# Expert rows by indirect DMA through a slot table, and a third full weight buffer, in one decoder layer with 32 experts

## The chip, the cores and the metric

The kernel runs on one core of one Trainium2 chip. The core has a matrix engine (TensorE, written PE; PEld is its weight load), a vector engine (DVE), an activation engine (ACT), GpSimd (POOL) and SyncE (SP), which issues DMAs. Transfers that SP, ACT and POOL issue run on the same 16 DMA engines. The metric is the device time of one execution in microseconds (us). Time before: median 947.78 us of 3 runs, 944.93 to 948.92. About 0.5% is what a measurement of this kernel can tell from no change.

## What is computed

One layer of a hybrid decoder: RMSNorm, one input projection, four parallel mixers, an output projection with a residual, then a second RMSNorm and a mixture of experts with a residual. 512 prompt tokens and 8 sample tokens pass through, 520 in all; everything is float32. The change concerns the mixture of experts and what stands just ahead of it. Each token picks one group of experts and two experts in it; there are 32 experts, each with a 1024x1024 matrix of gate and up columns (4 MB) and a 512x1024 matrix down (2 MB).

```python
D_MODEL = 1024; N_GROUPS = 4; EXP_PER_GROUP = 8; N_EXPERTS = 32; TOP_E = 2; D_EXPERT = 512
...
def moe_ffn(x, wg_r, bg_r, we_r, be_r, w_gu, w_down):
    ...
    gsel = jnp.argmax(lg, axis=-1)
    p_group = jnp.take_along_axis(pg, gsel[:, None], axis=-1)
    ...
    tv, ti = lax.top_k(le_g, TOP_E)
    gate = p_group * jax.nn.softmax(tv, axis=-1)
    eidx = gsel[:, None] * EXP_PER_GROUP + ti
    return expert_dispatch(xt, eidx, gate, w_gu, w_down).reshape(B_, L, D)
...
    # per expert e, over the tokens xi that chose it:
        a, b = jnp.split(xi @ w_gu[e], 2, axis=-1)
        return (jax.nn.silu(a) * b) @ w_down[e]
...
    return jax.ops.segment_sum(yb * buf_gate[:, None].astype(yb.dtype), buf_tok, num_segments=T)
```

## The kernel before

Every engine has its own instruction stream, written out by hand; semaphores (`S["..."]`, waited for with `wait_ge`) are the only order between streams. An engine works in the order of its stream, so what stands behind a wait waits too. Tokens lie on partitions in five tiles: four of 128 prompt tokens and one of 8 sample tokens. Large regions of SBUF (`reg_a`, `reg_b`, `reg_w`, `reg_h`, `reg_x`, `reg_y`, `reg_q`) are reused from stage to stage.

The work ahead of the experts ends with the output projection (weights in `reg_w`), the second norm (its result `h2` lies in `reg_h`), the router's logits and, on DVE, the choice of experts. `mask_bf` says which token chose which expert; PE multiplies it with triangular and full matrices of ones, and `pos` is then a token's place in its expert's list. An expert takes up to `CAP` = 64 tokens in one round; the number of rounds is computed on the chip (`n_rounds`), and in the profile it is one.

The expert loop on PE (`expert`, L1424 to L1452). A list of 64 tokens with 1024 numbers each is kept as 128 partitions of 512: the first half of a row on partitions 0 to 63, the second on 64 to 127, and matmuls come in pairs, one for each half of the array. For expert n PE does

- 16 matmul calls of gate and up (bank 2 or 3), in four parts; a part begins when its quarter of the weights has landed (`gu_loaded`), and its end frees that quarter (`gu_part_done`);
- 8 calls of `gather` for the expert after it: the tokens' rows are fetched by multiplying a one-hot matrix (made by DVE, `make_onehot`, L1876) with `h2`; the last 2 calls, of the tile with the sample tokens, stand after the next item;
- the transposition of `hid`, silu(gate) times up (ACT L1013, DVE L1925), which DVE copies into `hT` (L1929);
- 8 calls of the down projection with `hT`, and in the middle of them `turn_tokens`, 4 transpositions of the rows that `gather` fetched (ACT copies them out of the bank first), which DVE copies into `xe` (`copy_xe`, L1916).

A matmul call in float32 stands as two records in the profile. Line L1031 is the helper of all matmuls, L1034 that of all transpositions, L731 that of ACT's copies.

Weights: SP issues four DMAs of 1 MB for an expert's gate and up matrix (`load_gu`, L559) and one of 2 MB for the down matrix (`load_down`, L564). Three places hold gate and up matrices (`reg_a`, `reg_b`, `reg_w`), two hold down matrices (`reg_a`, `reg_b`). Experts 0 and 1 are loaded under the output projection, the gate and up matrix of expert 2 once the output projection has left `reg_w`. The third place is used for experts 2 and 5 alone; from expert 6 on the loop alternates between `reg_a` and `reg_b`. Each load waits for PE to have freed its place.

ACT copies an expert's result `y_out` and stores it in two DMAs into `expert_rows` in DRAM, 64 rows whether filled or not (L1022). After the last store POOL fetches, for every token, the rows of its two experts with ten indirect DMAs (L724; `slot_u` holds the row numbers), and DVE adds them to the residual, weighted by `gate` (L1943, ten operations); SP stores each finished tile.

## Time and profile before

| what | value |
|---|---|
| median of 3 runs | 947.78 us (944.93 to 948.92) |
| the profiled execution | 949.59 us |
| its span | 947.9 us |
| PE busy | 868.7 us, 92% |
| DVE, ACT, POOL busy | 242.0, 174.3, 65.1 us |
| mean granted clock of PE | 0.957 |
| DMA | 249.48 MB, 263 GB/s over the span |

The profiled execution took 949.59 us, 1.7 us more than its span and 1.8 us more than the median. PE's busy time counts a matmul from its issue to its modelled end, so full occupancy says that PE always had work queued, not that it could not be faster. From about 407 us to 917 us PE runs the expert loop; the DMA share (1.00 is all 16 DMA engines busy) and GB/s by stretch tell how the weights came in beside it. The order of instructions that is quoted below gives line, operation, out<-in and shape; a row with xN stands for N equal ones, and the rows ISA and REGISTER_ALU are an engine's own bookkeeping for loops and semaphores.

### The profile page before, as it was taken

The numbers are of one execution on the slowest core, as the hardware profiler recorded it, in microseconds if no ns is written. First come the engines' busy times: TensorE is split into PE (matmuls) and PEld (weight loads), VectorE is DVE, ScalarE is ACT, GpSimd is POOL, SyncE is SP. The second block draws the span as 40 slices with busy tenths as digits, with TensorE's granted clock in tenths as the row PEclk, the third lists the DMA queues.
The fourth block names the chain that finished last, engine by engine and source line by source line (L and its number), as shares of the span: only waits on it lengthen the run. The fifth ranks groups of instructions, "written<-read, shape, count | busy, mean of one in ns | idle before, by whom it ended". The sixth has DMA issues, their size and how long they took to land.

```text
span 947.9 us, 11251 instructions
## 1 busy us (share of the span) xinstructions
PE 868.7 (92%) x4270; PEld 439.6 (46%) x4270; DVE 242.0 (26%) x576; ACT 174.3 (18%) x386; POOL 65.1 (7%) x96
## 2 busy tenths in 40 slices
PE   4999899979889999599999999999999999999960
PEld 3787588848658455333333333333333333333320
DVE  3322004348668221611111111111111111110105
ACT  4113213021354301111111111111111111101100
POOL 6011000241100000000000000000000000000004
PEclk9999899989898999599999999999999999999995
DMA  9722833100600670459997999999999999999717
GB/s 300 122 62 67 265 126 95 50 19 1 268 1 1 264 293 4 174 194 410 401 381 284 397 412 400 425 411 415 396 426 405 422 396 424 406 423 409 289 27 265
DMA packets 69266, 249.48 MB, mean 263 GB/s; under 512 B 16772, under 2 KB 36115, under 8 KB 44619
## 3 DMA queue, kind: packets, MB, share of 16 engines
q1 hardware_dynamic: 62705, 234.12, 63.7%
q10 hardware_dynamic: 5314, 10.68, 3.0%
q0 software_dynamic: 1216, 4.26, 1.4%
q8 instruction: 20, 0.33, 0.1%
q14 instruction: 11, 0.09, 0.0%
...
## 4 chain that ended last, share of the span: by engine, by line
PE 83%; DVE 9%; DMA 2%; issue 2%; POOL 1%; ACT 1%; SPq 1%; POOLq 0%; ACTq 0%; DVEq 0%
PE bank L1031 76%; PE bank L1034 6%; POOL reg_a L724 1%; DMA reg_x<-in_x_prompt 1%; DMA reg_a<-expert_rows,slot_u 1%; DVE reg_a L1687 1%; DVE reg_a L1767 1%; DVE reg_a L1677 0%; DVE reg_x L1677 0%; DVE small L1728 0%; DMA reg_a<-in_state_win_kv 0%; POOL small L662 0%; DVE reg_a L1679 0%; DVE reg_a L1696 0%; POOLq L179 0%
## 5 line engine op out<-in xcount | busy, mean ns | idle before, releaser
L1031 PE MATMUL bank<-reg_a,reg_y 128*64 128x512 f32 x736 | 166.6, 594 | 0.9 <-DVE reg_y L1916 0.9
L1031 PE MATMUL bank<-reg_b,reg_y 128*64 128x512 f32 x736 | 166.5, 594 | 0.0
L1031 PE MATMUL bank<-reg_h,reg_y 128*64 128x512 f32 x660 | 156.2, 603 | 1.6 <-DVE reg_y L1876 1.6
L1031 PEld LDWEIGHTS bank<-reg_a,reg_y 128*64 128x64 f32 x736 | 51.8, 137 | 98.7 <-issue 96.5
L1031 PEld LDWEIGHTS bank<-reg_b,reg_y 128*64 128x64 f32 x736 | 51.8, 137 | 98.2 <-issue 96.0
L1031 PE MATMUL bank<-reg_b,reg_w 128*128 128x260 f32 x384 | 85.3, 383 | 0.0
L1031 PEld LDWEIGHTS bank<-reg_h,reg_y 128*64 128x64 f32 x660 | 45.1, 138 | 82.1 <-issue 78.2
L1925 DVE TENSOR_TENSOR reg_y<-reg_y,bank 128x256 f32<-128x256 f32 x32 | 13.5, 421 | 270.2 <-ACT reg_y L1013 270.2
L1031 PEld LDWEIGHTS bank<-reg_b,reg_w 128*128 128x128 f32 x384 | 72.7, 190 | 12.1 <-issue 1.1
L1031 PE MATMUL bank<-reg_w,reg_y 128*128 128x512 f32 (+2 forms) x256 | 75.8, 570 | 0.0
L731 ACT ACTIVATE reg_y<-bank 128x512 f32<-128x512 f32 x49 | 29.3, 597 | 213.8 <-PE bank L1031 213.8
L1031 PE MATMUL bank<-reg_w,reg_b 128*128 128x256 f32 (+2 forms) x320 | 60.5, 382 | 0.0
L1031 PEld LDWEIGHTS bank<-reg_w,reg_b 128*128 128x128 f32 (+1 forms) x320 | 50.8, 170 | 8.3 <-ACT reg_a L731 0.4
L724 POOL DMA_INDIRECT reg_a<-expert_rows,slot_u x10 | 13.5, 1350 | 543.8 <-ACTq L1025 541.1
L1034 PEld LDWEIGHTS bank<-small,reg_y 128*128 128x128 f32 (+3 forms) x209 | 25.3, 159 | 54.2 <-issue 52.3
L1031 PEld LDWEIGHTS bank<-reg_w,reg_y 128*128 128x128 f32 (+2 forms) x256 | 30.3, 157 | 39.9 <-issue 39.1
L1916 DVE COPY reg_y<-bank 128x512 f32<-128x512 f32 x33 | 22.9, 692 | 94.3 <-PE bank L1034 94.3
L1013 ACT ACTIVATE reg_y<-bank 128x256 f32<-128x256 f32 x32 | 12.3, 385 | 154.0 <-PE bank L1031 154.0
L1034 PE MATMUL bank<-small,reg_y 128*128 128x128 f32 (+3 forms) x209 | 39.9, 300 | 0.7 <-ACT reg_y L731 0.7
L1929 DVE COPY reg_y<-bank 128x256 f32<-128x256 f32 x32 | 13.6, 425 | 83.8 <-PE bank L1034 83.8
L662 POOL TENSOR_TENSOR small<-small 128x1 f32<-128x1 f32 (+4 forms) x18 | 20.2, 1126 | 199.2 <-DVE small L1821 68.1
L1034 PE MATMUL bank<-small,reg_h 128*128 128x128 f32 (+1 forms) x108 | 17.7, 315 | 16.0 <-DVE reg_h L1479 13.8
...
## 6 DMA issues: line engine op xcount, KB each, us to landing
reg_a<-in_exp_w_gu SPq DMA_DIRECT2D x60, 1024.0 KB, 12.1
reg_b<-in_exp_w_gu SPq DMA_DIRECT2D x60, 1024.0 KB, 12.4
reg_a<-in_exp_w_down SPq DMA_DIRECT2D x16, 2048.0 KB, 10.7
reg_b<-in_exp_w_down SPq DMA_DIRECT2D x16, 2048.0 KB, 10.5
reg_w<-in_w_in SPq DMA_DIRECT2D x9, 1024.0 KB, 10.4
reg_w<-in_exp_w_gu SPq DMA_DIRECT2D x8, 1024.0 KB, 11.8
...
expert_rows<-reg_y ACTq DMA_DIRECT2D x32, 128.0 KB, 7.7
```

Of the source, the lines that this page charges most:

```text
L662: eng.tensor_tensor(out, in_, minus_half[0:out.shape[0], 0:out.shape[-1]], ALU.pow).then_inc(S[s_done], 1)
L724: eng.indirect_dma_start(dst, None, y_dram[:, :], bass.IndirectOffsetOnAxis(ap=slot_u[0:ROWS[i], 5 * k + i:5 * k + i + 1], axis=0)).then_i ...
L731: return eng.activation(out, in_, ACT.Copy)
L1013: eng.activation(silu[b], bank[2 + b][:, 0:256], ACT.Silu).then_inc(S["silu_done"], 1)
L1031: return eng.matmul(out, lhsT, rhs, start=start, stop=stop, skip_group_check=True)
L1034: return eng.transpose(out, in_, ident[0:in_.shape[0], 0:in_.shape[0]])
L1687: link(eng.reciprocal(u, u))
L1767: eng.reciprocal(rs, rs).then_inc(S["nrm_made"], 1)
L1916: eng.tensor_copy(xe[b], bank[1][:, :].rearrange("p (j s n) -> p j s n", j=4, s=2)).then_inc(S["xe_made"], 1)
L1925: tt(hid[b], silu[b], bank[2 + b][:, 256:512], ALU.mult).then_inc(S["hid_made"], 1)
L1929: eng.tensor_copy(hT[b], bank[4 + b][:, 0:256].rearrange("p (k s) -> p k s", k=2)).then_inc(S["hT_made"], 1)
```

## The change

- PE no longer fetches tokens with one-hot matmuls. ACT stores `h2` into DRAM (`ffn_in`) tile by tile. DVE makes a table of which token's half-row belongs on which of the 128 partitions for each expert (`find_slots`, ten small bf16 matmuls `slot_table`, `rows_of_slots`); partitions without a token get a number that the bounds check drops. POOL fetches an expert's rows from `ffn_in` into `xe_rows` with one indirect DMA (`gather`).
- Results go from `y_out` into `expert_rows` with one indirect DMA an expert, issued by POOL (`scatter`); `expert_rows` now has a row for each token and choice, and at the end plain DMAs bring it back (`combined_rows`, by SP and ACT), two rows a token at once.
- `reg_h`, free once `h2` is stored and transposed, becomes the third place for down matrices. Expert e uses place e mod 3; the down matrix of expert 2 is loaded ahead of the loop too.
- Constants for the table are added to POOL's first work.

The expert loop on PE, two experts in a row of the loop of before (names: `small` holds the identity matrix of a transposition, `reg_h` is `h2`):

```order
L1031 MATMUL bank<-reg_a,reg_y 64x512 x16
L1435 REGISTER_ALU
L1031 MATMUL bank<-reg_h,reg_y 64x512 x8
L1034 MATMUL bank<-small,reg_y 128x128 x2
L1031 MATMUL bank<-reg_h,reg_y 64x512 x2
L1442 ISA
L1031 MATMUL bank<-reg_a,reg_y 64x512 x4
L1034 MATMUL bank<-small,reg_y 128x128 x4
L1031 MATMUL bank<-reg_a,reg_y 64x512 x4
```

The same loop of now, its second and third expert (`reg_h` is here a down matrix):

```order
L1068 MATMUL bank<-reg_b,reg_y 64x512 x16
L1443 REGISTER_ALU
L1071 MATMUL bank<-small,reg_y 128x128 x6
L1068 MATMUL bank<-reg_b,reg_y 64x512 x8
L1459 REGISTER_ALU
L1463 ISA
L1068 MATMUL bank<-reg_w,reg_y 64x512 x16
L1071 MATMUL bank<-small,reg_y 128x128 x6
L1068 MATMUL bank<-reg_h,reg_y 64x512 x8
```

The ten calls of `gather` are gone; the four transpositions of the next expert's rows moved from the middle of the down projection to just behind gate and up, ahead of the two of `hid`.

DVE ahead of the loop, before, from the mask of chosen experts to the first one-hot matrices:

```order
L1866 CAST mask_bf<-reg_y 128x160
L1869 COPY reg_y<-bank 128x160
L1872 SCALAR_TENSOR_TENSOR reg_q<-reg_y 128x5x32
L1873 TENSOR_SCALAR reg_q<-reg_q 128x5x32
L1876 TENSOR_TENSOR reg_y<-small,reg_q 128x320 x2
```

The same place now, up to the matrix for `slot_table` (128x1280) and the first step of the round count:

```order
L1895 CAST mask_bf<-reg_y 128x160
L1897 TENSOR_SCALAR reg_q<-reg_y,small 128x10x32
L1898 TENSOR_TENSOR reg_q<-reg_y,small 128x5x32
L1899 TENSOR_TENSOR reg_q<-reg_y,small 128x5x32
L1900 MEMSET reg_q 128x5x16
L1901 CAST reg_q<-reg_y 128x5x32
L1904 COPY reg_y<-bank 128x160
L1906 TENSOR_TENSOR reg_y<-reg_y 128x320
L1907 TENSOR_REDUCE reg_q<-reg_y 128x10
L1911 TENSOR_TENSOR reg_q<-small,reg_q 128x1280
L1930 TENSOR_REDUCE reg_y<-bank 128x1
```

Five operations on the token numbers came in ahead of the copy of `pos`, and the places of the tokens (L1906, L1907) moved ahead of the loop's first fetch.

POOL behind the norms, before (`slot_u` holds row numbers, `reg_a` takes the rows):

```order
L717 TENSOR_LOAD n_rounds
L717 ISA x2
L718 UNCONDITIONAL_BRANCH
L718 ISA
L724 DMA reg_a<-expert_rows,slot_u 128x1024 x2
L724 DMA reg_a<-expert_rows,slot_u 8x1024 x2
L724 DMA reg_a<-expert_rows,slot_u 128x1024 x6
```

And now, for the first two of 32 experts (`reg_q` holds the row numbers, `reg_y` the fetched rows and one of the two result buffers):

```order
L736 TENSOR_LOAD n_rounds
L736 ISA x2
L747 UNCONDITIONAL_BRANCH
L747 ISA
L741 DMA reg_y<-ffn_in,reg_q 128x512 x2
L755 ISA
L741 DMA reg_y<-ffn_in,reg_q 128x512
L758 REGISTER_ALU
L745 DMA expert_rows<-reg_y,reg_q 2080x512
L755 REGISTER_ALU
L741 DMA reg_y<-ffn_in,reg_q 128x512
L758 REGISTER_ALU
```

Ten indirect DMAs after the loop became 64 inside it, a fetch for expert e+2 and a return for expert e in turn.

The core of the diff:

```diff
-        down_w = [r.t[:, 8192:12288].rearrange("p (s c n) -> p s c n", s=2, c=2) for r in (reg_a, reg_b)]
+        down_w = [r.t[:, at:at + 4096].rearrange("p (s c n) -> p s c n", s=2, c=2) for r, at in ((reg_a, 8192), (reg_b, 8192), (reg_h, 0))]
...
+        h2_dram = nc.dram_tensor("ffn_in", [T, D], F32, kind="Internal").ap()
+        y_dram = nc.dram_tensor("expert_rows", [2 * T, D], F32, kind="Internal").ap()
...
+        USES = [11, 11, 10]
+        h2_halves = h2_dram.rearrange("t (s n) -> (t s) n", s=2)
+        y_halves = y_dram.rearrange("t (s n) -> (t s) n", s=2)
+        y_pairs = y_dram.rearrange("(k t) d -> t k d", k=2)
+        def combined_rows(eng, t):
+            q = ROWS[t]
+            dst = reg_a.t[0:q, 2 * t * D:2 * t * D + 2 * D].rearrange("p (k d) -> p k d", k=2)
+            eng.dma_start(dst, y_pairs[COL[t]:COL[t] + q]).then_inc(y_back[t], 16)
...
-                for e, g in ((3, 0), (4, 1), (5, 2), (6, 0), (7, 1)):
-                    load_gu(e, g, first + e - 2)
-                    load_down(e - 1, (e - 1) % 2, first + e - 2)
-                with eng.Fori(0, (N_EXP - 8) // 2) as i:
-                    for k in range(2):
-                        e = 2 * i + 7 + k
-                        load_down(e, 1 - k, first + e - 1)
-                        load_gu(e + 1, k, first + e)
-                load_down(N_EXP - 1, 1, first + N_EXP - 2)
+                with eng.Fori(1, N_EXP // 3) as i:
+                    for g in range(3):
+                        e = 3 * i + g
+                        load_gu(e, g, first + e - 2)
+                        load_down(e, g, first + e - 2)
+                for e in range(N_EXP - N_EXP % 3, N_EXP):
+                    load_gu(e, e % 3, first + e - 2)
+                    load_down(e, e % 3, first + e - 2)
...
+            eng.wait_ge(S["h2_stored"], 16 * NTILE)
+            eng.wait_ge(bank_full[bank_of["hTb3"]], turn_of["hTb3"] + 1)
+            load_down(2, 2)
...
+            eng.wait_ge(S["round_scattered"], rounds)
+            for t in COMBINE_TILES[0::2]:
+                combined_rows(eng, t)
...
+            eng.wait_ge(S["h2_stored"], 16 * NTILE)
+            def gather(e):
+                idx = bass.IndirectOffsetOnAxis(ap=row_of[:, e:e + 1], axis=0)
+                eng.indirect_dma_start(xe_rows[e % 2], None, h2_halves, idx, bounds_check=2 * T - 1, oob_is_err=False).then_inc(x_gathered[e % 2], 16)
+            def scatter(e):
+                idx = bass.IndirectOffsetOnAxis(ap=row_of[:, N_EXP + e:N_EXP + e + 1], axis=0)
+                eng.indirect_dma_start(y_halves, idx, y_out[e % 2], None, bounds_check=4 * T - 1, oob_is_err=False).then_inc(y_scattered[e % 2], 16)
...
-                eng.sem_inc(S["gather_begun"], 1)
-                for i in COMBINE_TILES:
-                    for k in range(2):
-                        dst = reg_a.t[0:ROWS[i], (2 * i + k) * D:(2 * i + k + 1) * D]
-                        eng.indirect_dma_start(dst, None, y_dram[:, :], bass.IndirectOffsetOnAxis(ap=slot_u[0:ROWS[i], 5 * k + i:5 * k + i + 1], axis=0)).then_inc(rows_gathered[k][i], 16)
+                n = N_EXP * r
+                eng.wait_ge(S["idx_made"], r + 1)
+                eng.sem_inc(S["gather_asked"], 1)
+                gather(0)
+                gather(1)
+                for e in range(N_EXP):
+                    if e + 2 < N_EXP:
+                        eng.wait_ge(S["xe_turned"], n + e + 1)
+                        eng.sem_inc(S["gather_asked"], 1)
+                        gather(e + 2)
+                    eng.wait_ge(S["y_copied"], n + e + 3)
+                    eng.sem_inc(S["scatter_asked"], 1)
+                    scatter(e)
+                for b in range(2):
+                    eng.wait_ge(y_scattered[b], 16 * (N_EXP // 2) * (r + 1))
+                    eng.sem_inc(S["scatter_asked"], 1)
+                eng.sem_inc(S["round_scattered"], 1)
...
+                eng.wait_ge(S["h2_made"], n + 1)
+                eng.dma_start(h2_dram[COL[i]:COL[i] + r], h2[0:r, i, :]).then_inc(S["h2_stored"], 16)
...
+            def expert(e, n, b, reused=None):
+                eng.wait_ge(S["gu_done"], n + 1)
+                eng.activation(silu[b], bank[2 + b][:, 0:256], ACT.Silu).then_inc(S["silu_done"], 1)
+                eng.wait_ge(S["down_done"], n + 1)
+                if reused is not None:
+                    eng.wait_ge(y_scattered[b], reused)
+                copy(y_out[b], bank[6 + b][:, :]).then_inc(S["y_copied"], 1)
...
-                        copy(y_out[b], bank[6 + b][:, :]).then_inc(S["y_copied"], 1)
-                        eng.wait_ge(S["y_copied"], n + 3)
-                        for s in range(2):
-                            eng.dma_start(y_dram[bass.ds(e * CAP, CAP), 512 * s:512 * s + 512], y_out[b][CAP * s:CAP * s + CAP, :]).then_inc(y_stored[b], 16)
...
-            def gather(b, tiles):
-                for t in tiles:
-                    for s in range(2):
-                        ins = mm(bank[0][64 * s:64 * s + 64, :], onehot[b][:, t, :], h2[:, t, 512 * s:512 * s + 512], t == 0, t == NTILE - 1)
-                if t == NTILE - 1:
-                    ins.then_inc(S["gathered"], 1)
...
+            def slot_table(made):
+                eng.wait_ge(S["in_slot_made"], made)
+                for m_ in range(10):
+                    ins = mm(bank[0][:, 0:96], in_slot[:, m_, :], ids[:, m_ // 5, m_ % 5].rearrange("p f e -> p (f e)"), m_ == 0, m_ == 9)
+                ins.then_inc(S["table_made"], 1)
+            def turn_tokens(b, gathered):
+                eng.wait_ge(x_gathered[b], gathered)
                 for j in range(4):
-                    ins = turn(bank[1][:, 128 * j:128 * j + 128], x_tok[:, 128 * j:128 * j + 128])
+                    ins = turn(bank[1][:, 128 * j:128 * j + 128], xe_rows[b][:, 128 * j:128 * j + 128])
                 ins.then_inc(S["xe_turned"], 1)
...
-                eng.wait_ge(S["onehot_made"], n + 2)
-                gather(1 - b, range(4))
+                if gathered is not None:
+                    turn_tokens(1 - b, gathered)
                 eng.wait_ge(S["hid_made"], n + 1)
                 for k in range(2):
                     ins = turn(bank[4 + b][:, 128 * k:128 * k + 128], hid[b].rearrange("p (f k) -> p f k", k=2)[:, :, k])
                 ins.then_inc(S["xt_turned"], 1)
-                gather(1 - b, [4])
-                eng.wait_ge(down_loaded[b], down_loads)
+                eng.wait_ge(down_loaded[g], loads)
                 eng.wait_ge(S["hT_made"], n + 1)
                 eng.wait_ge(S["y_copied"], n + 1)
                 for s_in in range(2):
-                    if s_in == 1:
-                        eng.wait_ge(S["x_tok_made"], n + 2)
-                        turn_tokens()
                     for k in range(2):
...
+            ts(ids[:, :, :, 0], oh, row_one, None, ALU.mult)
+            tt(ids[:, 0, :, 1], oh[:, 0], tile_iota.unsqueeze(2).to_broadcast([128, 5, N_EXP]), ALU.mult)
+            tt(ids[:, 1, :, 1], oh[:, 1], tile_iota.unsqueeze(2).to_broadcast([128, 5, N_EXP]), ALU.mult)
+            eng.memset(ids[:, 0, :, 2], 0.0)
+            eng.tensor_copy(ids[:, 1, :, 2], oh[:, 1])
...
-            link(stt(posm[:, :, 0:N_EXP], pos, 1.0, mask, ALU.add, ALU.mult))
-            link(ts(posm[:, :, 0:N_EXP], posm[:, :, 0:N_EXP], -1.0, None, ALU.add))
-            def make_onehot(n, b):
-                tt(onehot[b], cap_iota.unsqueeze(1).to_broadcast([128, 5, CAP]), posm[:, :, bass.ds(n, 1)].to_broadcast([128, 5, CAP]), ALU.is_equal).then_inc(S["onehot_made"], 1)
-            make_onehot(0, 0)
-            make_onehot(1, 1)
...
+            def find_slots(at):
+                tt(in_slot, cap_iota.unsqueeze(1).to_broadcast([128, 10, 2 * CAP]), at.unsqueeze(2).to_broadcast([128, 10, 2 * CAP]), ALU.is_equal).then_inc(S["in_slot_made"], 1)
+            def rows_of_slots(made, steps):
+                eng.wait_ge(S["table_made"], made)
+                row, tile, second = [bank[0][:, 32 * f:32 * f + 32] for f in range(3)]
+                eng.tensor_copy(slot_no, row).then_inc(S["idx_steps"], 1)
+                eng.wait_ge(S["idx_steps"], steps + 1)
+                stt(slot_v[:, 0], tile, 128.0, slot_no, ALU.mult, ALU.add).then_inc(S["idx_steps"], 1)
+                eng.wait_ge(S["idx_steps"], steps + 2)
+                ts(slot_no, slot_v[:, 0], 0.0, 8192.0, ALU.is_equal, ALU.mult)
+                stt(slot_v[:, 1], second, float(T), slot_v[:, 0], ALU.mult, ALU.add).then_inc(S["idx_steps"], 1)
+                eng.wait_ge(S["idx_steps"], steps + 3)
+                stt(slot_v, slot_v, 2.0, slot_no.unsqueeze(1).to_broadcast([128, 2, N_EXP]), ALU.mult, ALU.add).then_inc(S["idx_steps"], 1)
+                eng.wait_ge(S["idx_steps"], steps + 4)
+                ts(row_of, slot_v.rearrange("p x e -> p (x e)"), half_less2, None, ALU.add).then_inc(S["idx_made"], 1)
+            find_slots(pk10)
...
+            rows_of_slots(1, 0)
...
+                n = N_EXP * r
+                eng.wait_ge(S["idx_made"], r + 1)
+                ts(pk_next, pk_next, float(-CAP), None, ALU.add).then_inc(S["next_at"], 1)
+                eng.wait_ge(S["next_at"], r + 1)
+                find_slots(pk_next)
+                copy_xe(n, 0)
...
+                eng.wait_ge(S["round_scattered"], r + 1)
+                rows_of_slots(r + 2, 4 * r + 4)
+                eng.sem_inc(S["round_open"], 1)
+            for n, t in enumerate(COMBINE_TILES):
+                q = ROWS[t]
+                eng.wait_ge(y_back[t], 16)
+                for k in range(2):
+                    ins = stt(x1[0:q, t, :], reg_a.t[0:q, (2 * t + k) * D:(2 * t + k + 1) * D], gate[0:q, k, t:t + 1], x1[0:q, t, :], ALU.mult, ALU.add)
+                    ins.then_inc(S["half_added" if k == 0 else "y_tile_done"], 1)
+                    if k == 0:
+                        eng.wait_ge(S["half_added"], n + 1)
```

## Rows read from the trace of the kernel before

**Rows 1.** The page: span, and the chain that ended last by line.

```profile
span 947.9 us, 11251 instructions
...
PE bank L1031 76%; PE bank L1034 6%; POOL reg_a L724 1%; DMA reg_x<-in_x_prompt 1%; DMA reg_a<-expert_rows,slot_u 1%; DVE reg_a L1687 1%; DVE reg_a L1767 1%; DVE reg_a L1677 0%; DVE reg_x L1677 0%; DVE small L1728 0%; DMA reg_a<-in_state_win_kv 0%; POOL small L662 0%; DVE reg_a L1679 0%; DVE reg_a L1696 0%; POOLq L179 0%
```

**Rows 2.** Timeline of one expert: start us, us, engine, line, operation, count [idle before].

```profile
605.20 3.60 PE L1031 MATMUL bank<-reg_h,reg_y 128*64 128x512 f32 x16
...
605.83 0.42 DVE L1925 TENSOR_TENSOR reg_y<-reg_y,bank 128x256 f32<-128x256 f32 x1 [8.47 <-ACT reg_y L1013]
...
608.73 0.50 PE L1034 MATMUL bank<-small,reg_y 128*128 128x128 f32 x2
...
611.89 0.66 PE L1034 MATMUL bank<-small,reg_y 128*128 128x128 f32 x4
...
614.25 7.04 PE L1031 MATMUL bank<-reg_b,reg_y 128*64 128x512 f32 x32
...
621.12 3.60 PE L1031 MATMUL bank<-reg_h,reg_y 128*64 128x512 f32 x16
```

**Rows 3.** Busy time by stretch, with granted clock, DMA share, GB/s.

```profile
core 0: us, PE busy (x) PEld busy (x) DVE busy (x) ACT busy (x) POOL busy (x), PEclk, DMA share, GB/s
...
320.00:340.00 20.00, 20.00 (x68) 9.14 (x67) 7.13 (x8) 2.58 (x6) 1.10 (x2) 1.00 1.01 426
...
380.00:390.00 10.00, 7.86 (x40) 7.32 (x40) 2.94 (x9) 1.84 (x4) 0.48 (x1) 0.60 0.94 395
390.00:400.00 10.00, 2.00 (x24) 1.20 (x26) 8.80 (x57) 0.43 (x2) 0.00 (x0) 0.50 0.01 2
...
500.00:600.00 100.00, 100.00 (x468) 34.41 (x466) 12.34 (x25) 13.92 (x22) 0.00 (x0) 1.00 0.96 386
...
700.00:800.00 100.00, 100.00 (x468) 34.21 (x462) 12.47 (x26) 13.71 (x22) 0.00 (x0) 1.00 1.01 412
```

**Rows 4.** DMA queues (packets, MB, share) and issues (count, KB each, us to landing).

```profile
q10 hardware_dynamic: 5314, 10.68, 3.0%
q0 software_dynamic: 1216, 4.26, 1.4%
...
reg_a<-in_exp_w_gu SPq DMA_DIRECT2D x60, 1024.0 KB, 12.1
...
reg_a<-in_exp_w_down SPq DMA_DIRECT2D x16, 2048.0 KB, 10.7
```

**Rows 5.** Timeline ahead of the loop and at its first matmuls, columns as rows 2.

```profile
395.18 0.56 DVE L1863 TENSOR_TENSOR reg_y<-reg_y,small 128x160 f32<-128x160 f32 x2
...
396.14 0.24 DVE L1866 CAST mask_bf<-reg_y 128x160 bf16<-128x160 f32 x1
...
398.07 0.89 DVE L1876 TENSOR_TENSOR reg_y<-small,reg_q 128x320 f32<-128x320 f32 x2
...
401.19 0.15 DVE L1891 CAST n_rounds<-reg_y 128x1 int32<-128x1 f32 x1
...
407.28 7.09 PE L1031 MATMUL bank<-reg_a,reg_y 128*64 128x512 f32 x32 [0.87 <-DVE reg_y L1916]
...
409.25 5.48 SPq L559 DMA_DIRECT2D reg_a<-in_exp_w_gu  x4
```

**Rows 6.** Timeline of the end, columns as rows 2.

```profile
916.88 0.60 ACT L731 ACTIVATE reg_q<-bank 128x512 f32<-128x512 f32 x1 [3.57 <-PE bank L1031]
...
921.55 1.25 POOL L724 DMA_INDIRECT reg_a<-expert_rows,slot_u  x1 [541.07 <-ACTq L1025]
923.11 0.94 POOL L724 DMA_INDIRECT reg_a<-expert_rows,slot_u  x1 [0.30 <-issue]
...
926.22 1.28 DVE L1943 SCALAR_TENSOR_TENSOR reg_x<-reg_a,reg_q,reg_x 128x1024 f32<-128x1024 f32 x1 [10.06 <-DMA reg_a<-expert_rows,slot_u]
...
928.64 1.99 POOL L724 DMA_INDIRECT reg_a<-expert_rows,slot_u  x1 [0.31 <-issue]
...
943.51 1.28 DVE L1943 SCALAR_TENSOR_TENSOR reg_x<-reg_a,reg_q,reg_x 128x1024 f32<-128x1024 f32 x1 [1.24 <-DMA reg_a<-expert_rows,slot_u]
```

191 lines of the change are left out of this document (78 added, 113 removed).

## The prediction

> **What bounds the kernel now.** I read the page first: the chain that ended last is 76% matmuls, more than half of it the expert loop [rows 1]. Then the timeline of one expert: the same matmuls stand 15.92 us apart (605.20 to 621.12) [rows 2], and 407.28 + 32 x 15.92 = 916.7 us is where the loop ends, 0.2 us before ACT's last copy [rows 5, 6]. PE never waits in it. Third, busy time by stretch, which shows that the transfers have hardly more room: from 700 to 800 us the DMA share is 1.01 at 412 GB/s, PE busy 100.00 [rows 3]. An expert's weights are 4 x 1024 + 2048 KB = 6.29 MB [rows 4], its stored rows 0.26 MB, and 6.55 MB in 15.92 us is that 412. So PE is the bound and the transfers come a few per cent behind. Around the loop stand 407 us ahead of it, which the change touches only at the end, and 31.0 us behind it (916.88 to 947.9) [rows 1, 6].
>
> **PE's work per expert.** Gate and up are 32 records in 621.12 - 614.25 = 6.87 us, 0.2147 each [rows 2]. The ten calls of gather are 20 records, 4.29 us: 15.92 - 4.29 = 11.63. But the gather covered two waits. Until hid is made 1.05 us pass after the last gate-and-up matmul (605.20 to 606.25) [rows 2]; the four moved transpositions (0.66) cover most, 0.4 shows, and since they no longer stand in the middle of the down projection nothing waits there. Behind the transposition of hid the last gather calls (4 records, 0.86) covered the copy into hT; now 0.6 to 1.0 us is open, as DVE copies xe first. Together about 13.0 us an expert (bounds 11.6 to 13.6). If the weights were there, 32 experts would take 416 us.
>
> **The transfers take over.** The weights alone ran at 426 GB/s from 320 to 340 us [rows 3]: 6.29 MB in 14.8 us. Rows: 520 tokens in two experts each are 1040 rows, 32.5 an expert, fetched and returned in halves of 2 KB, so 130 packets if the bounds check drops the empty ones at no cost. Queue q10, which carries the stores of before, took 3.0% of 16 engines x 947.9 us for 5314 packets, 86 ns each [rows 4]: 130 x 86 ns / 16 = 0.7 us. That is 15.5 us an expert, the lower bound. The upper one is the stretch 700 to 800, with 128 such packets in each 15.92 us and no DMA engine idle [rows 3]: 15.9. I take 15.8, nearer to the stretch with this mix of traffic. PE with 13.0 waits for weights from about expert 9 on.
>
> **Where the gain is.** Hardly in 15.92 against 15.8, but in the count: experts 0 to 2 lie in SBUF when the loop begins (down 2 is new, and loads while DVE routes, 390 to 400 us, DMA share 0.01 [rows 3]), so 29 experts are paid at the transfers' rate, and PE is not 16 us behind them at the end.
>
> **Ahead of the loop.** The mask is made at 396.38 [rows 5].
> - Five operations on token numbers: two 160 wide take 0.56 [rows 5], so 1.3 us, while PE makes pos: 397.7.
> - Copy of pos, product, reduction: 0.35 + 0.5 + 0.5, estimated from the 320 wide ones [rows 5]: 399.1.
> - The 1280 wide find_slots: two 320 wide take 0.89 [rows 5], so 1.6: 400.7.
> - Round count, beside the ten matmuls: five steps like n_rounds (0.15 and a gap) [rows 5], 1.1: 401.8. Then rows_of_slots, six steps of about 0.2: 403.1.
> - Two paths to the first transposition. POOL: 4.7 us from an indirect DMA's start to the first sum that used it (921.55 to 926.22) [rows 6], 407.8. DVE: gates 1.1, a register load (no row; 0.5 taken, 0 to 1.9 possible), find_slots again 1.7, then PE's second table about 1.0 and a latency: 407.9. Then 0.66 [rows 2] and the copy into xe, 0.8.
> The loop begins at 409.9 instead of 407.28 (bounds 408.5 to 412). The gather of before also woke the clock; granted 0.50 from 390 to 400 us [rows 3], PE now begins cold, and its first quarter takes 1.7 us more. First buffer free: before 1.97 after the loop's start [rows 5], now 409.9 + 1.97 + 1.7 = 413.6.
>
> The five stores of h2 stand on ACT's queue behind copies that wait for PE anyway, and 2.1 MB of them ride beside loads that nothing awaits before 407 us; SP waits for them ahead of down 2 with nothing else to issue. POOL's extra constants, about 0.7 us before its first power, are put at 0.3 here and dropped.
>
> **The sum.** 413.6 + 2.2 until bytes land (4.67 less POOL's 1.25 and half a MB's 1.2 [rows 6]) + 29 x 15.8 = 874.0. The last down projection, 16 records, 3.4, and a latency: ACT's copy at 877.9 instead of 916.88, 39.0 us earlier. Behind it: copy 0.6, scatter on POOL 1.25 and 3.4 to land, 5.3 in all. Plain loads: issue and latency 2.7, 5 us until the first tile is there (it shares the engines with a second queue), then DVE is the bound: ten sums of 1.28 [rows 6], 12.8, and the last store 3.1 (944.79 to 947.9). 28.9 instead of 31.0, 2.1 gained; bounds 26 to 32, as loads land earlier or later. Span 947.9 - 39.0 - 2.1 = 906.8; the execution 949.59 gives 908.5, and against the median of 947.78, which is 1.8 lower, **906.7, so 907 us**.
>
> **A rule against it.** Of POOL's ten indirect DMAs one that DVE left alone took 0.94 us, one beside DVE's sums 1.99 [rows 6]. The Trainium skill, page "SBUF — State Buffer", section "Who interferes with whom", says that a vector operation in a two-port mode keeps GpSimd from the port it writes descriptors through. By it the first gather and the last scatter would each cost about 1.1 us more, and the sum would be 909; inside the loop POOL has 13 us to spare and nothing changes.
>
> **Rivals.**
> - *Empty rows are not free* (slower). Were all 256 half-rows of the two indirect DMAs moved, and each cost what a packet of POOL's queue q0 did, 1.4% x 947.9 x 16 / 1216 = 175 ns [rows 4], rows would take 2.8 us an expert on every DMA engine: 14.8 + 2.8 = 17.6, and 907 + 29 x 1.8 = 959. It decides from 907 + 29 x 1.4, that is 17.2 us an expert. For it: POOL's queue has never run beside the weights here. Against: q0's packets were twice as long.
> - *Transfers at their slower stretch.* From 500 to 600 us 386 GB/s [rows 3]: 6.29 MB in 16.3, with rows 17.0: 907 + 35 = 942, a gain of only 0.6%. Against: the share there was 0.96, so the engines were not full. Half of that, 16.4, gives 924.
> - *The clock.* PE will wait some 3 of 15.8 us. From 380 to 390 us it was busy 7.86 of 10 and got 0.60 [rows 3], which stands for part of the time at 1.2 GHz. If the down projection always ran at that level, 3.4 us more make 16.4 an expert and PE the bound: 924. Worse is not stable, since a PE that falls behind has no gaps. The Trainium skill, page "TensorE: Matmul & The Clock Gate", section "HAM oscillation", describes this for waits on DMA, each stretch of work starting cold; the stretch just quoted agrees.
> - *A late gather.* Gather e+2 stands on POOL's queue behind scatter e-1, which waits for ACT's copy; it is needed after gate and up of e+1, some 25 us later. At 12.1 us, the longest median landing under load [rows 4], it is hidden; from 25 on it is not. Priced with the first rival.
> - *No change.* The loads were nearly full before, so if 29 paid experts cost 17.1 each, 945.
>
> **Chances.** Forecast (15.4 to 16.1 us an expert, 893 to 916) 0.62; slower transfers or the clock (916 to 943) 0.23; a tail and rate better than taken (below 893) 0.03; no change (943 to 952) 0.04; slower by the first rival 0.08. Faster 0.62 + 0.23 + 0.03 = 0.88, within 0.5% (about what a measurement of this kernel can tell) 0.04, slower 0.08. Range: low end 15.5 an expert (-8.7), an early loop and a short tail (-7): 891; high end 938, inside the slower cases, which leaves out some 0.16.
>
> **What would show it.** In the profile after: DMA share at 1.0 from about 415 to 872 us, gate and up at intervals of 15.8 us with PE idle 2 to 3 us ahead of the down projection; SP's waits for PE shrinking to the first experts; the loop's start at 409 to 412; from ACT's last copy to the end about 29 us, DVE's sums without gaps. Wrong if PE is still busy throughout, if PE waits for x_gathered (the four transpositions late), or if the interval is above 17 us.

## The result

The changed kernel takes 908.51 us (median of 4 runs, 906.86 to 912.16), the kernel before 946.36 us in the runs beside it: ratio 0.9593, 95% interval 0.9557 to 0.9629. A second set of runs gave 909.86 us and 0.9603 (0.9586 to 0.9620). Forecast were 907 us and a range of 891 to 938. The profiled execution spans 905.1 us, where 906.8 was forecast.

### The profile page after: what moved, and what is told of

Same layout as the page of the kernel before. It is cut to its first block, busy times and chain, and to the rows that moved or that the text cites. A ratio compares the mean times of both kernels' runs of the same rounds, so it can differ in the third digit from the quotient of the medians.

```text
span 905.1 us, 9802 instructions
## 1 busy us (share of the span) xinstructions
PE 752.3 (83%) x3626; PEld 404.3 (45%) x3626; DVE 226.2 (25%) x540; ACT 135.3 (15%) x338; POOL 118.9 (13%) x154
## 4 chain that ended last, share of the span: by engine, by line
PE 40%; SPq 34%; DVE 11%; DMA 9%; issue 4%; ACT 2%; POOL 0%; DVEq 0%; ACTq 0%; POOLq 0%
PE bank L1068 37%; SPq L571 28%; DMA reg_b<-in_exp_w_down 7%; SPq L576 5%; PE bank L1071 3%; DVE reg_x L1983 1%; DMA reg_x<-in_x_prompt 1%; DVE reg_a L1718 1%; DMA reg_a<-expert_rows 1%; DVE reg_a L1798 1%; DVE reg_a L1708 1%; DVE reg_x L1708 0%; DVE small L1759 0%; POOL small L681 0%; DVE reg_a L1710 0%
## 5 line engine op out<-in xcount | busy, mean ns | idle before, releaser
L1068 PE MATMUL bank<-reg_a,reg_y 128*64 128x512 f32 x528 | 127.2, 634 | 16.1 <-DMA reg_a<-in_exp_w_down 12.9
L1068 PE MATMUL bank<-reg_b,reg_y 128*64 128x512 f32 x528 | 122.2, 608 | 21.9 <-DMA reg_b<-in_exp_w_down 17.2
L1068 PE MATMUL bank<-reg_w,reg_y 128*64 128x512 f32 (+2 forms) x512 | 134.2, 581 | 4.3 <-DMA reg_w<-in_exp_w_gu 4.3
L1957 DVE TENSOR_TENSOR reg_y<-reg_y,bank 128x256 f32<-128x256 f32 x32 | 13.5, 421 | 421.3 <-ACT reg_y L1047 421.3
L1068 PEld LDWEIGHTS bank<-reg_w,reg_y 128*64 128x64 f32 (+2 forms) x512 | 49.2, 146 | 82.3 <-issue 65.1
L1068 PE MATMUL bank<-reg_b,reg_w 128*128 128x260 f32 x384 | 85.3, 383 | 0.0
L1068 PEld LDWEIGHTS bank<-reg_a,reg_y 128*64 128x64 f32 x528 | 41.2, 145 | 92.7 <-issue 75.6
L1068 PEld LDWEIGHTS bank<-reg_b,reg_y 128*64 128x64 f32 x528 | 39.9, 140 | 94.8 <-issue 64.6
L1068 PEld LDWEIGHTS bank<-reg_b,reg_w 128*128 128x128 f32 x384 | 72.7, 190 | 12.1 <-issue 1.1
L1068 PE MATMUL bank<-reg_h,reg_y 128*64 128x512 f32 x160 | 48.9, 768 | 19.1 <-DMA reg_h<-in_exp_w_down 17.4
L1068 PE MATMUL bank<-reg_w,reg_b 128*128 128x256 f32 (+2 forms) x320 | 60.5, 382 | 0.0
L1068 PEld LDWEIGHTS bank<-reg_w,reg_b 128*128 128x128 f32 (+1 forms) x320 | 50.8, 170 | 8.3 <-ACT reg_a L771 0.4
L1071 PEld LDWEIGHTS bank<-small,reg_y 128*128 128x128 f32 (+3 forms) x205 | 25.2, 161 | 45.8 <-issue 25.5
L745 POOL DMA_INDIRECT expert_rows<-reg_y,reg_q x16 | 16.3, 1018 | 208.7 <-ACT reg_y L771 198.0
L745 POOL DMA_INDIRECT expert_rows<-reg_q x16 | 16.2, 1015 | 193.8 <-ACT reg_q L771 193.8
L741 POOL DMA_INDIRECT reg_y<-ffn_in,reg_q x32 | 34.4, 1074 | 34.8 <-DVE reg_q L1926 23.7
L1068 PEld LDWEIGHTS bank<-reg_h,reg_y 128*64 128x64 f32 x160 | 14.1, 174 | 46.4 <-issue 27.6
L771 ACT ACTIVATE reg_q<-bank 128x512 f32<-128x512 f32 (+3 forms) x31 | 15.9, 527 | 115.1 <-PE bank L1068 111.2
L1071 PE MATMUL bank<-small,reg_h 128*128 128x128 f32 (+1 forms) x108 | 17.0, 306 | 15.8 <-DVE reg_h L1510 13.5
```

What stands on the lines that cost most here:

```text
L741: eng.indirect_dma_start(xe_rows[e % 2], None, h2_halves, idx, bounds_check=2 * T - 1, oob_is_err=False).then_inc(x_gathered[e % 2], 16)
L745: eng.indirect_dma_start(y_halves, idx, y_out[e % 2], None, bounds_check=4 * T - 1, oob_is_err=False).then_inc(y_scattered[e % 2], 16)
L771: return eng.activation(out, in_, ACT.Copy)
L1068: return eng.matmul(out, lhsT, rhs, start=start, stop=stop, skip_group_check=True)
L1071: return eng.transpose(out, in_, ident[0:in_.shape[0], 0:in_.shape[0]])
L1957: tt(hid[b], silu[b], bank[2 + b][:, 256:512], ALU.mult).then_inc(S["hid_made"], 1)
```

## The profile after

The page first: the chain that ended last, of which the matmuls' helper (L1031, now L1068) was 76% [rows 1].

```profile
span 905.1 us, 9802 instructions
...
PE 40%; SPq 34%; DVE 11%; DMA 9%; issue 4%; ACT 2%; POOL 0%; DVEq 0%; ACTq 0%; POOLq 0%
PE bank L1068 37%; SPq L571 28%; DMA reg_b<-in_exp_w_down 7%; SPq L576 5%; PE bank L1071 3%; DVE reg_x L1983 1%; DMA reg_x<-in_x_prompt 1%; DVE reg_a L1718 1%; DMA reg_a<-expert_rows 1%; DVE reg_a L1798 1%; DVE reg_a L1708 1%; DVE reg_x L1708 0%; DVE small L1759 0%; POOL small L681 0%; DVE reg_a L1710 0%
```

The helper is down to 37%; SP's weight loads (L571, L576) and the landing of a down matrix have its place. That SP stands there for a third, and not a DMA, I read as a full queue: an issue of 1 MB took 0.33 us on SP in the loop's first 40 us and 1.9 to 6.4 us from 500 us on, while in e2 and e3 below, where PE paces the loads, it stays at 0.33 to the end. Busy time by stretch, columns as in [rows 3], agrees:

```profile
410.00:420.00 10.00, 9.24 (x36) 3.03 (x32) 1.39 (x3) 0.39 (x1) 0.00 (x0) 0.80 0.72 247
420.00:440.00 20.00, 18.94 (x89) 7.75 (x91) 1.50 (x4) 1.58 (x3) 3.92 (x4) 1.00 0.98 391
...
500.00:600.00 100.00, 86.75 (x390) 32.41 (x386) 10.10 (x21) 6.87 (x14) 15.50 (x16) 0.97 1.02 420
600.00:700.00 100.00, 80.68 (x340) 26.61 (x340) 8.66 (x18) 5.89 (x12) 13.12 (x13) 0.93 1.01 420
700.00:800.00 100.00, 79.79 (x340) 26.68 (x338) 10.10 (x21) 6.28 (x13) 12.27 (x12) 0.93 1.02 420
```

From 500 to 600 us the transfers were at 386 GB/s with PE at 100.00; now they stand at 420 GB/s throughout and PE is at 80 to 87. One expert on PE, from its last quarter of gate and up to the next expert:

```profile
603.10 1.94 PE L1068 MATMUL bank<-reg_w,reg_y 128*64 128x512 f32 x8 [0.56 <-DMA reg_w<-in_exp_w_gu]
604.97 0.66 PE L1071 MATMUL bank<-small,reg_y 128*128 128x128 f32 x4
605.98 0.50 PE L1071 MATMUL bank<-small,reg_y 128*128 128x128 f32 x2 [0.35 <-DVE reg_y L1957]
609.34 6.64 PE L1068 MATMUL bank<-reg_h,reg_y 128*64 128x512 f32 x16 [2.87 <-DMA reg_h<-in_exp_w_down]
615.82 7.03 PE L1068 MATMUL bank<-reg_a,reg_y 128*64 128x512 f32 x32
```

PE waits 2.87 us for the down matrix, and 0.56 for the last quarter of gate and up. The gate and up of the expert after that (615.82) runs through, since by then its quarters have landed. The down projection took 6.64 us, where 16 records of this shape took 3.60 [rows 2]: the granted clock was at its lower level, 1.2 GHz, from 608.6, still in the wait, to 615.4. The end of the program (columns as [rows 2], the rows that answer to [rows 6]):

```profile
880.27 0.60 ACT L771 ACTIVATE reg_q<-bank 128x512 f32<-128x512 f32 x1 [6.33 <-PE bank L1068]
881.73 0.98 POOL L745 DMA_INDIRECT expert_rows<-reg_q  x1 [12.42 <-ACT reg_q L771]
884.22 1.42 SPq L476 DMA_DIRECT2D reg_a<-expert_rows  x3
...
889.35 12.64 DVE L1983 SCALAR_TENSOR_TENSOR reg_x<-reg_a,reg_q,reg_x 128x1024 f32<-128x1024 f32 x10 [3.76 <-DMA reg_a<-expert_rows]
```

The ten sums are one row now, 12.64 us without a gap; between ACT's last copy and the end lie 24.8 us instead of 31.0.

## Experiments

The theory under test: after the first few experts the loop is bound by the bytes on the DMA engines, so its length is the bytes that are still to come when it begins, over 420 GB/s; PE's relief matters only because it puts PE under that. The rivals: PE's own waits and its clock, POOL's indirect DMAs, SP's issuing, or third buffers in rotation. "Interval" is the mean distance of an expert's silu product on DVE (L1957) from expert 12 to 28: 15.92 us before, 15.83 in the changed kernel. "Landing" is that of the last weights, 876.53 us in the changed kernel, and the copy is ACT's last, 880.27.

**e1_no_rows.** The rows' bytes taken out of the loop.

```diff
-                eng.indirect_dma_start(xe_rows[e % 2], None, h2_halves, idx, bounds_check=2 * T - 1, ...
+                eng.indirect_dma_start(xe_rows[e % 2], None, h2_halves, idx, bounds_check=0, ...
-                eng.indirect_dma_start(y_halves, idx, y_out[e % 2], None, bounds_check=4 * T - 1, ...
+                eng.indirect_dma_start(y_halves, idx, y_out[e % 2], None, bounds_check=0, ...
```

> Edit: in the loop the bounds of all 64 indirect DMAs are set so low that every row but number 0 is dropped, and the plain loads at the end read ffn_in instead; so the rows of the experts are left out, all else stays. Theory (the DMA engines bound the loop): only the weights are left, 6.29 MB an expert at the 426 GB/s of the weights alone is 14.8 to 15.0 us instead of 15.8, 29 x 0.9 = 26 us less: about 882 us, ratio to before 0.93, DMA share still 1.0. Rival (PE with its waits and its half clock bounds the loop, or SP's issuing of the weights does): the interval stays at 15.8, 908 us, ratio 0.96.

Measured: 887.42 us, ratio 0.9368 (0.9352 to 0.9384). Interval 14.94 (its first step is still PE's own, 12.73; the other 15 are 15.08 on the mean), and from the first load to the last landing 442.1 us instead of 464.5: 22.4 / 29 = 0.77 us an expert are the rows' (forecast 0.7). The stretch from 500 to 800 us, the changed kernel's first and then this one's:

```profile
500.00:800.00 300.00, 247.21 (x1066) 85.70 (x1064) 28.86 (x60) 19.03 (x39) 40.88 (x40) 0.94 1.02 420
```

```profile
500.00:800.00 300.00, 256.42 (x1130) 90.02 (x1128) 30.32 (x63) 20.60 (x42) 42.01 (x42) 0.97 1.02 418
```

About the same GB/s with fewer bytes to move, and a shorter loop: the transfers are the bound. SP issues as many loads as in the changed kernel, so its issuing is not. Whether an engine's time is its own or that of the memory behind it, these runs do not tell apart. The result stays 5 us above the expected 882: 418 GB/s are 15.05 us an expert, where 14.8 to 15.0 were expected.

One thing the theory leaves out shows when the end of the loop is set beside that of the changed kernel. There the transfers fade out (first fence, columns as in [rows 3]), here they stop at once (second):

```profile
840.00:860.00 20.00, 17.04 (x74) 5.83 (x70) 2.50 (x6) 1.37 (x3) 1.02 (x1) 0.91 1.02 421
860.00:870.00 10.00, 8.53 (x34) 2.77 (x36) 0.38 (x1) 0.60 (x1) 1.00 (x1) 0.83 0.83 349
870.00:877.00 7.00, 4.44 (x22) 1.40 (x20) 0.84 (x2) 0.38 (x1) 0.00 (x0) 1.00 0.19 78
```

```profile
840.00:850.00 10.00, 9.07 (x44) 2.69 (x40) 0.00 (x0) 0.60 (x1) 1.00 (x1) 1.00 1.02 419
850.00:854.00 4.00, 1.44 (x8) 0.42 (x6) 0.84 (x2) 0.38 (x1) 0.00 (x0) 1.00 0.44 180
```

With the rows, most of the 16 engines are done by about 870 us, and the last landing comes at 876.53; without the rows, all end within some 4 us, with the last landing at 853.85. So the rows do not load the engines alike, and the pace is that of the engines that come last: an expert's 6.56 MB at 420 GB/s would be 15.6 us, not 15.83. What stands idle at the end is an estimated 7 us of all engines (share 0.83 and 0.19 instead of 1.02), against 2 in this run, so some 5 of the 22.4 us are this and not bytes. Which engines they are, and why, is not shown.

**e2_quarter_gu.** Weights' bytes halved, so that PE alone is left.

```diff
-                for part in range(GU_PARTS):
+                for part in range(GU_PARTS if free is None else 1):
...
-                        eng.wait_ge(gu_loaded[g][part], loads)
+                        eng.wait_ge(gu_loaded[g][part], loads if part == 0 else 16)
```

> Edit: from expert 3 on only the first of four quarters of a gate and up matrix is loaded, PE uses what lies in the other three places; all instructions on PE, ACT, DVE and POOL stay. Theory: the loop falls to PE's own 12.5 us an expert (the first experts of the changed kernel, whose weights lay ready), 408.2 + 3.4 for the cold start + 32 x 12.53 = 812.6, plus tail 24.8, about 840 us, ratio 0.888, granted clock 1.00 throughout, DMA share about 0.55. Rival (the indirect DMAs of POOL, the landing of the fetched rows or the loop's semaphores set the pace, not the weights' bytes): above 870 us, with PE waiting for x_gathered.

Measured: 841.02 us, ratio 0.8879 (0.8864 to 0.8893), interval 12.52. The stretch from 500 to 800 us and all of PE's waits in it (line, releaser, us in total, times, longest):

```profile
PE bank L1068 <- issue: 13.5, 24, 0.6
PE bank L1071 <- DVE reg_y L1957: 8.3, 24, 0.3
...
500.00:800.00 300.00, 278.20 (x1296) 113.97 (x1294) 34.70 (x72) 23.55 (x48) 48.13 (x47) 1.00 0.68 259
```

No wait for a weight or a fetched row; the two that are left are those that the one-hot gather had covered, 0.56 and 0.35 us in each expert. With POOL's indirect DMAs all in place, these do not set the pace. So PE's work is 12.52 us (forecast 13.0), and 3.3 of 15.8 us are PE's slack.

**e3_fill24, e4_fill12.** PE's work put back, whole and by half.

```diff
+            def fill(b, pairs):
+                for _ in range(pairs):
+                    for s in range(2):
+                        mm(bank[0][64 * s:64 * s + 64, 96:512], xe[b][:, 0, 0, :], x1[:, 0, 0:416], True, True)
...
+                fill(b, 5)      # e4: 2
                 eng.wait_ge(S["hid_made"], n + 1)
...
+                fill(b, 1)
                 eng.wait_ge(down_loaded[g], loads)
```

> Edit: PE gets back matmuls of about the length of the former gather, 12 calls (24 records) of 128x64 by 128x416 an expert, 24 x 0.175 = 4.2 us, 10 calls ahead of the transposition of hid and 2 behind it; the results are not used. Buffers, transfers and the indirect DMAs stay. Theory: PE needs 12.5 + 4.2 - 0.9 (the two waits it covers) = 15.8 to 15.9 us an expert again, and since PE's time counts for 32 experts and not 29, the time is 408.2 + 2 + 32 x 15.9 + 24.8 + 1.8 = 945 us, ratio 1.00, PE busy without gaps. Rival (the gain comes from the third buffers and the loads ahead of the loop, whatever PE does): 908 us, ratio 0.96.

> Edit: half of that, 6 calls (12 records, 2.1 us) an expert, 4 ahead of the transposition of hid and 2 behind it; results not used. Theory: PE needs 13.7 to 14.6 us, still under the 15.8 of the transfers: 908 us within 5, ratio 0.955 to 0.965, PE's waits down to about 1.5 us an expert, granted clock back to 1.00. Rival (PE's finishing late keeps places occupied and so delays transfers, or the half clock costs time): the first makes it slower, over 915; the second makes it faster, under 900, as the clock no longer falls.

Measured: e3 944.75 us, ratio 0.9968 (0.9954 to 0.9982); e4 910.58 us, 0.9604 (0.9588 to 0.9621). The same stretch, e3 and then e4:

```profile
500.00:800.00 300.00, 300.00 (x1482) 108.88 (x1482) 27.49 (x57) 18.65 (x38) 38.92 (x38) 1.00 1.01 416
```

```profile
500.00:800.00 300.00, 285.22 (x1342) 96.01 (x1340) 29.62 (x62) 20.01 (x41) 40.96 (x40) 1.00 1.02 420
```

This pair carries the case. In e3 PE's interval is 15.81 us, that of the changed kernel 15.83, and yet 36 us lie between them: PE pays its interval from expert 0 on, 32 times, the transfers pay it from expert 3 on. In e4 PE needs 13.72 us, the granted clock no longer falls (1.00 against 0.94), and the time is that of the changed kernel: within the loop neither the lower clock in the down projections nor PE's waits cost anything that shows.

**e5_two_down.** The third place for down matrices undone.

```diff
-        down_w = [... for r, at in ((reg_a, 8192), (reg_b, 8192), (reg_h, 0))]
+        down_w = [... for r, at in ((reg_a, 8192), (reg_b, 8192))]
...
+                        load_gu(e, j % 3, first + e - 2)
+                        load_down(e - 1, j % 2, first + e - 2)
```

> Edit: the third place for down matrices is undone. Expert e uses place e mod 2, the down matrix of expert 2 isn't loaded ahead of the loop, and loads are issued in the order gate and up of e, down of e-1, as before the change; three places for gate and up stay. Theory (the loop is a queue of bytes; what a buffer gives is what it lets be loaded ahead): 2.1 MB more are paid at 420 GB/s, 5.0 us: 913 us (911 to 917), ratio 0.965, interval still 15.8. Rival (the third place keeps the transfers going through the whole loop): over 0.5 us an expert, from 925 us on, with DMA share under 1.0.

Measured: 922.12 us, ratio 0.9750 (0.9714 to 0.9785): a miss, 5 us above the range. Not the rival: interval 15.91, DMA share 1.01 to 1.02. The last weights landed at 881.32, 4.8 us later than in the changed kernel, which is what 2.1 MB cost. But the copy came 11.3 us behind the landing instead of 3.7:

```profile
876.44 3.65 PE L1067 MATMUL bank<-reg_a,reg_y 128*64 128x512 f32 x16 [1.45 <-DMA reg_a<-in_exp_w_down]
879.92 7.04 PE L1067 MATMUL bank<-reg_b,reg_y 128*64 128x512 f32 x32
887.90 0.51 PE L1070 MATMUL bank<-small,reg_y 128*128 128x128 f32 x2 [0.94 <-DVE reg_y L1956]
888.97 3.65 PE L1067 MATMUL bank<-reg_b,reg_y 128*64 128x512 f32 x16 [0.56 <-issue]
```

Gate and up 31 had landed by 871.15, but ahead of it in PE's order stands down 30, which had been queued behind it. PE then has an expert of its own left when the transfers are done.

**e9_swap, e12_order.** The places of e5; only the order of the last loads differs.

```diff
                 for e in range(27, N_EXP):     # e12; e9: for expert 31 alone
-                    load_gu(e, e % 3, first + e - 2)
                     load_down(e - 1, (e - 1) % 2, first + e - 2)
+                    load_gu(e, e % 3, first + e - 2)
```

> Two places for down matrices as in e5_two_down, which took 922 us where 913 was expected, though its interval stayed 15.84 and DMA share 1.01. Edit: of the last loads only the order is changed, down 30 ahead of gate and up 31 instead of behind it. Theory (the 2.1 MB more cost 5 us, and the rest of the miss is at the end: there down 30 landed behind gate and up 31, so PE had down 30, all of gate and up 31 and down 31 still to do after the transfers were nearly over, and the last copy came 11.3 us after the last landing instead of 3.7): that falls back to 3.7 and the time to 922.1 - 7.6 = 914.5 us, ratio 0.966. Rival (the two places cost through the whole loop): stays at 922, ratio 0.975.

> As e9_swap, but the order is turned from expert 26 on: down 26 ahead of gate and up 27, down 27 ahead of gate and up 28, and so on to the end. In e9 the pinch had only moved one expert forward: down 29 landed behind gate and up 30 at 860.2 us, and from there PE had two and a half experts to do at its own 12.5 us, more than the transfers still needed (to 877). Theory (the place of a down matrix in the queue costs PE up to one gate and up, and PE makes up 15.8 - 12.5 = 3.3 us with each expert): five experts are enough for the 7.6 us, and the time is that of the changed kernel plus 2.1 MB, 5.0 us: 914 us, ratio 0.965. Rival (what e9 left, 3.6 us, is the two places' own): 918.5, ratio 0.970.

Measured: e9 918.57 us, ratio 0.9696 (0.9674 to 0.9719), a miss as well, since only about half of what e5 lost came back; e12 915.16 us, 0.9646 (0.9627 to 0.9664), as expected. In e9 down 29 is the last load that PE waits for (860.28); from there to the copy (889.0) it works at its own pace. In e12 landing is at 883.16, the copy 5.4 us later, 1.7 of which are the lower clock (the last down projection took 5.35 us instead of 3.65). So the third place is worth 2.1 MB of loads ahead, 5 us, and the order in which it lets the loads stand another 7.

**e6_two_places.** From expert 3 on two places alternate, for both matrices.

```diff
+                with eng.Fori(0, (N_EXP - 6) // 2) as i:
+                    for k in range(2):
+                        e = 2 * i + 5 + k
+                        load_gu(e, k, first + e - 1)
+                        load_down(e, k, first + e - 1)
```

> Edit: third places for gate and up and for down serve expert 2 alone; from expert 3 on two places alternate, so a load waits for the expert two ahead of it and not three. Loads ahead of the loop are those of the changed kernel. Theory: once PE waits for weights the queue always holds the rest of one expert and all of the next, so two places keep it full; only experts 3 to 6, when PE is still ahead of nothing it must wait for, can leave gaps of 1 to 4 us: 908 to 916 us, interval 15.8 from 500 us on. Rival (three full places in rotation are what the gain comes from): DMA share under 0.97 in the loop and over 925 us.

Measured: 911.44 us, ratio 0.9644 (0.9610 to 0.9678), interval 15.82. The gap is where it was expected, and nowhere behind it:

```profile
440.00:460.00 20.00, 18.19 (x87) 7.45 (x85) 2.89 (x6) 1.36 (x3) 2.05 (x2) 1.00 0.82 320
460.00:500.00 40.00, 37.28 (x176) 15.29 (x174) 4.33 (x9) 3.54 (x7) 6.72 (x7) 1.00 1.01 418
```

So rotation through three places is worth some 4 us at the beginning (469.1 us from the first load to the last landing instead of 464.5), which the intervals of the two times are too wide to separate; in the loop two places keep the queue full (DMA share 1.01 to 1.02 from 500 to 800 us).

**e7_empties.** Partitions without a token fetch a row too.

```diff
+                ts(slot_g, slot_v[:, 0], 0.0, row_one, ALU.is_equal, ALU.mult)
...
+                stt(slot_v[:, 0], slot_v[:, 0], 2.0, slot_g, ALU.mult, ALU.add)
...
+                ts(row_of[:, 0:N_EXP], slot_v[:, 0], half_less2, 0.0, ALU.add, ALU.max)
```

> Edit: partitions without a token fetch a half-row of their own from ffn_in instead of a dropped one (the return stays as it is), so each fetch moves 128 half-rows of 2 KB instead of 65 on average. Theory (bytes bound the loop, dropped rows cost next to nothing): 63 packets of 73 ns on 16 engines are 0.29 us an expert, 29 x 0.29 = 8.4 us: 917 us, ratio 0.968, interval 16.1. Rival (a dropped row costs what a moved one does, or rows fill gaps that the weights leave): 908 us, ratio 0.960.

Measured: 915.01 us, ratio 0.9647 (0.9612 to 0.9681; its low end lies inside both intervals of the changed kernel). First load to last landing 471.5 us instead of 464.5, 0.24 us an expert (0.29 expected); the interval, 15.92 where 16.1 was expected, shows less of it. The row of POOL's queue (packets, MB, share of 16 engines' span) in the changed kernel, in this one and in e1:

```profile
q0 software_dynamic: 5120, 8.54, 2.6%
```

```profile
q0 software_dynamic: 5120, 12.66, 3.6%
```

```profile
q0 software_dynamic: 5120, 0.04, 0.4%
```

A dropped row still has its part in a packet, as the count doesn't change, but one with hardly a byte. By the packets in the changed kernel's trace two half-rows share one: with both of them, 4096 bytes, it took 164 ns, with both dropped, 8 bytes, 10 ns. The 4.12 MB more took 161 us on the 16 engines, and 161 us / 2012 rows = 80 ns each.

**e8_better, e10_better2.** What is not transfers made shorter.

```diff
             slot_table(1)
+            for _ in range(4):      # e10: 6
+                mm(bank[7][:, 0:256], ident, x1[:, 0, 0:256], True, True)
...
+                for s in range(2):
+                    eng.dma_start(down_w[e % 3][:, s], down_dram[e:e + 1, :, s]...).then_inc(S["last_half"] if s == 0 else down_loaded[e % 3], 16)
...
+            for k in range(2):
+                eng.dma_start(dst[:, k, :], y_dram[T * k + COL[t]:T * k + COL[t] + q]).then_inc(y_back[t] if k == 0 else x_loaded[t], 16)
```

> Three edits meant to shorten what is not transfers: (1) four matmuls on data of no use (128x128 by 128x256) behind the first slot table, so that PE works while the first rows are fetched and the clock is up when expert 0 begins; (2) the last expert's down matrix is loaded in two halves and PE starts on the first; (3) the rows come back in ten plain DMAs, one for each tile and choice. Theory: (1) expert 0's gate and up take 7.0 instead of 10.0 us and the first place comes free 1.7 us earlier, so the transfers start and end 1.5 to 2 us earlier; (2) the last matmuls end 1.8 us earlier; (3) the first sum starts about 1 us earlier: 903.5 to 905, ratio 0.955. Rival (the transfers' start does not depend on PE's clock, or the end on the last matmuls): 908.5.

> As e8_better, but six instead of four matmuls of no use ahead of the loop. In e8 the four ended at 406.5 us, PE stood still for 1.9 us before the second slot table, and the granted clock, up at 406.9, fell again from 410.35 to 413.76, in expert 0. Theory: six fill the 5.6 us between the two slot tables, the clock stays at 1.00 once it is up, expert 0's gate and up take 7.0 us (10.0 in the changed kernel, 8.8 in e8); with what e8 gains at the end (1.3 us behind the last landing, 0.8 us in the tail) 903 us, ratio 0.953. Rival (the clock falls again all the same, in the 0.9 us in which PE waits for xe): as e8, 905 us.

> The changed kernel, unchanged, beside the two others on the same chip: ratio 0.9593 as before, within 0.3%, that is 908 us where the kernel before takes 947. If e10 is really faster, by theory 5 us, the two ratios must lie apart by 0.005.

Measured: e8 905.21 us, ratio 0.9555 (0.9525 to 0.9585); e10 903.54 us (902.53 to 904.54), 0.9539 (0.9522 to 0.9555); the changed kernel beside e10 909.86 us, 0.9603 (0.9586 to 0.9620). The intervals of e10 and the changed kernel lie apart: e10 beats both. Its PE ahead of the loop and at its start:

```profile
398.74 0.96 PE L1073 MATMUL bank<-reg_q 128*128 128x96 bf16 x10 [3.52 <-DVE reg_y L1939]
399.50 5.34 PE L1073 MATMUL bank<-reg_x,small 128*128 128x256 f32 x12
405.13 0.60 PE L1073 MATMUL bank<-reg_q 128*128 128x96 bf16 x10 [0.30 <-DVE reg_q L1920]
405.57 0.62 PE L1076 MATMUL bank<-small,reg_y 128*128 128x128 f32 x4
407.12 7.09 PE L1073 MATMUL bank<-reg_a,reg_y 128*64 128x512 f32 x32 [0.93 <-DVE reg_y L1962]
```

Gate and up of expert 0 take 7.09 us (9.97 in the changed kernel). From the first slot table to the first load of the loop 10.5 us pass instead of 13.1, and from the landing to the copy 2.8 instead of 3.7 (5.4 in e11's profile, where the clock fell ahead of the last down projection). Edit (3) gave nothing that shows: the tail is 25.4 us, in e8 24.0, in the changed kernel 24.8 and 25.2. Of the 6.3 us between the medians the profiles show 2.6 at the start and 0.9 to 2.5 at the end of the loop; the rest stays open, since the part ahead of the experts alone moves by some us between executions (the first slot table stands at 395.43, 398.98 and 401.97 us in three profiles).

## Why the prediction was right, step by step

- *The bound changes hands.* Right, and shown from both sides (e1, e2). PE runs at 12.52 us an expert up to expert 10 and waits for weights from there on (forecast: about 9).
- *PE's expert.* 12.52 us (e2; the first experts of the changed kernel read the same), forecast 13.0. The two waits behind silu and the copy into `hT` were taken as up to 1.4 us and are 0.9.
- *The rate.* Forecast 29 x 15.8 + 2.2 = 460.4 us from the first free place to the last landing; measured 876.53 - 412.04 = 464.5. The steady interval, 15.83, is right. Of the 4.1 us 2.4 are at the beginning, a term that the sum lacked: the weights of expert 3 have landed at 432.41 us, 20.4 after the first load and not 18.0. From 410 to 440 us the transfers are not yet full (share 0.72, then 0.98), because PE frees gate and up of expert 0 long before its down matrix, whose load follows at 423.97 us. The other 1.7 us are the pace of the landings from there on, 15.86 us an expert and not 15.8. The 15.8 itself was a choice between two bounds. It came out because the weights alone take 15.08 us (e1), not the 14.8 of the working, and the rows 0.77, of which a part is not bytes but engines that come last.
- *The start of the loop.* 408.18 us, forecast 409.9; first load 412.04, forecast 413.6. The clock was cold as forecast (gate and up 9.97 us instead of 7.09), and e10 got it back.
- *The tail.* 24.8 us, forecast 28.9 and below its bounds of 26 to 32: the mis-sized term. The sums are 12.64 us (12.8), the last store 3.1. From the copy to the issue of the loads 3.95 us (5.3: the last return landed within 2.5 us of its start, where 4.7 was taken from a fetch), from there to the first sum 5.1 (7.7, of which no row showed either part; 1 MB of the first tile alone at 420 GB/s is an estimated 2.5 us, and with the 2.7 of issue and latency 5.2, as if it had the engines to itself).
- *The sum.* 1.6 us earlier at the start, 4.1 more in the transfers, 4.1 less in the tail: the errors cancel, which is luck, and 907 against 908.5 looks better than the terms were.
- *The port.* POOL's second fetch, beside DVE's `find_slots`, took 2.25 us; the first took 1.31, the median of all 32 is 1.03, the last return took 0.98. The fetch that was slowed is one that nobody waits for: it cost nothing of the 2.2 us by which the sum would have risen. The Trainium skill, page "SBUF — State Buffer", section "Who interferes with whom", gives `tensor_tensor`, which `find_slots` is, no two-port mode; it has it contend with GpSimd's reads when both inputs lie in SBUF, as they do here.
- *Rivals.* Empty rows are free but for 10 ns a packet of two (e7, e1). The late fetch did not occur: no wait for `x_gathered` stands among PE's waits in the loop. The lower clock occurred, 13 times between 560 and 865 us for 3.4 to 6.8 us each, with 13 of the 20 waits of 1.5 to 2.9 us for a down matrix. In the loop it cost nothing, since PE had the time (e4); with the last down projection it can: in e11, the changed kernel again, that took 5.29 us instead of 3.65. The Trainium skill, page "TensorE: Matmul & The Clock Gate", section "HAM oscillation", describes such a fall in waits for DMA, there with every stretch of work. The 386 GB/s of the stretch from 500 to 600 us before were not the engines' limit: with places coming free early they ran at 420.
